# Band attention scores: 128-row products over zero-filled key maps in place of 64-row products

## The reference

```
proj = rmsnorm(h) @ w_in
q (8 heads of 64), k (2 heads of 64), v (2 heads of 64) = the first 768 columns of proj
scores = einsum("bnqkgd,bnskd->bnkgqs", q blocks, k bands) * 64 ** -0.5
scores = scores + bias, masked to |key - query| <= 128
probs  = softmax([scores, sink])[..., :-1]
out    = einsum("bnkgqs,bnskd->bnqkgd", probs, v bands)
```

## Time and profile before

| | |
|---|---|
| median of 3 runs | 2589.55 us (2588.72 to 2590.06) |
| span of the profiled execution | 2587.0 us |
| median less that span (the execution's own time is not printed) | 2.55 us |
| PE busy | 2482.1 us, 96% of the span |
| PE's share of the chain that ended last | 93% |
| share of line L632 (scores) in that chain | 2% |
| the band, 103.8 to 412.9 us | 309.1 us |

### The profile page before, as it was taken

How to read it: one execution, slowest core, us unless ns; L and a number is a source line. 1 busy time by engine, 2 the same in 40 slices (tenths; PEclk the granted TensorE clock), 3 DMA queues, 4 the chain that set the end, 5 groups by cost and what they waited for, 6 DMA issues and landing times.

```text
span 2587.0 us, 33189 instructions
## 1 busy us (share of the span) xinstructions
PE 2482.1 (96%) x13182; PEld 2079.7 (80%) x13182; DVE 991.7 (38%) x1474; ACT 723.0 (28%) x1147; POOL 689.0 (27%) x423
## 2 busy tenths in 40 slices
PE   7999998799989999999999999999999999999997
PEld 5777776699967788888888887888888788887886
DVE  4155633545443421311312235113333353557533
ACT  4134354222321200100101121135444113655022
POOL 2211111343322333433333332311111231111321
PEclk8999998799989999999999998999999999999998
DMA  5211111322331111111111112633441346424422
GB/s 188 96 33 50 33 51 65 74 56 56 119 136 43 34 50 47 49 49 49 49 49 49 49 49 91 219 94 94 115 114 42 133 156 162 116 80 147 146 90 90
DMA packets 247261, 220.54 MB, mean 85 GB/s; under 512 B 42513, under 2 KB 219447, under 8 KB 245608
## 3 DMA queue, kind: packets, MB, share of 16 engines
q1 hardware_dynamic: 225416, 164.36, 22.3%
q10 hardware_dynamic: 21728, 54.57, 5.9%
HBM read 161.12 MB, written 59.87 MB: 85 GB/s over the span
## 4 chain that ended last, share of the span: by engine, by line
PE 93%; DVE 2%; DMA 1%; ACT 1%; POOL 0%; issue 0%; POOLq 0%; ACTq 0%; DVEq 0%; SPq 0%; PEldq 0%; PEld 0%
PE PS L282 40%; PE PS L301 18%; PE PS L1770 4%; PE PS L2420 3%; PE PS L418 3%; PE PS L1725 3%; PE PS L1976 2%; PE PS L632 2%; PE PS L1268 2%; PE PS L1262 2%; PE PS L653 1%; PE PS L1965 1%; PE PS L2259 1%; PE PS L1279 1%; PE PS L641 1%; PE PS L410 1%
## 5 line engine op out<-in xcount | busy, mean ns | idle before, releaser
L253 POOL CAST Wh<-Wraw 128x1024 fp32r<-128x1024 f32 x145 | 151.7, 1046 | 1518.5 <-PE PS L282 643.1
L255 POOL TENSOR_TENSOR Wl<-Wraw,Wh 128x1024 fp32r<-128x1024 f32 x145 | 377.6, 2604 | 20.9
L1644 ACT ACTIVATE rbuf<-PS 128x1024 f32<-128x1024 f32 x32 | 32.9, 1028 | 495.3 <-PE PS L282 484.8
L282 PE MATMUL PS<-Fh,Wh 128*128 128x512 f32 x512 | 157.6, 389 | 0.0
L282 PE MATMUL PS<-Fl,Wh 128*128 128x512 f32 x512 | 157.6, 389 | 0.0
L282 PE MATMUL PS<-Fh,Wl 128*128 128x512 f32 x512 | 157.6, 389 | 0.0
L282 PE MATMUL PS<-XAh,Wh 128*128 128x512 f32 x440 | 140.2, 400 | 8.8 <-POOL Wl L255 6.0
L301 PE MATMUL PS<-XAh,Wh 128*128 128x512 f32 x328 | 136.0, 415 | 2.1 <-POOL Wl L255 2.1
L282 PE MATMUL PS<-XAl,Wh 128*128 128x512 f32 x440 | 136.6, 392 | 0.0
L282 PE MATMUL PS<-XAh,Wl 128*128 128x512 f32 x440 | 136.4, 391 | 0.0
L301 PE MATMUL PS<-XAl,Wh 128*128 128x512 f32 x328 | 135.7, 414 | 0.0
(11 more groups left out here) (429 smaller groups left out, 5419.2 us busy)
## 6 DMA issues: line engine op xcount, KB each, us to landing
Wraw<-in_w_in SPq DMA_DIRECT2D x67, 512.0 KB, 4.1
Wraw<-in_w_ffn_in SPq DMA_DIRECT2D x32, 512.0 KB, 4.0
Wraw<-in_w_ffn_out SPq DMA_DIRECT2D x32, 512.0 KB, 4.0
x_scr<-hT SPq DMA_DIRECT2D x2, 4096.0 KB, 14.2
Wraw<-in_w_out SPq DMA_DIRECT2D x16, 512.0 KB, 4.1
gate_scr<-gbuf ACTq DMA_DIRECT2D x16, 512.0 KB, 2.7
gin<-gate_scr ACTq DMA_DIRECT2D x8, 1024.0 KB, 7.1
xtok<-in_x SPq DMA_DIRECT2D x4, 1024.0 KB, 8.5
```

Source lines behind the costliest of these rows:

```text
L253: pool.tensor_copy(Wh[:, slot], Wraw[:, slot])
L255: pool.tensor_tensor(Wl[:, slot], Wraw[:, slot], Wh[:, slot].bitcast(F32), ALU.subtract).then_inc(w_ready, 1)
L282: mm = pe.matmul(PS[:, 2 * slot + b, :], w[:, slot, k], x[:, b * 512:(b + 1) * 512], start=(c == 0 and m == 0), stop=(c == len(xs) - 1 and ...
```

## The change

The key tile is no longer kept whole. Two maps `kz` of 128 rows are made: map 0 has key head 0 in rows 0 to 63 and zeros in rows 64 to 127, map 1 zeros in rows 0 to 63 and key head 1 in rows 64 to 127. A score product takes the whole query tile (two heads) as stationary operand and the map of its key head as moving operand: the other head meets zeros. The result is the same sum. VectorE writes the zeros, after the split of the activations, and ScalarE waits for them before it copies the keys, now in two instructions of 64 rows. Values move to a tile of their own, `vT`. The semaphore `eps_ok` is renamed `filled` and counts to 3.

```diff
-        attT = sb("attT", [P, 6, S], F32, R + 48)
+        attT = sb("attT", [P, 4, S], F32, R + 48)
+        kz = sb("kz", [P, 2, S], F32, R + 64)
+        vT = sb("vT", [P, S], F32, R + 32)
...
-                    mm = pe.transpose(PS[:, 6 + half, t * P:(t + 1) * P], attT[:, 5, (4 * half + t) * P:(4 * half + t + 1) * P],
+                    mm = pe.transpose(PS[:, 6 + half, t * P:(t + 1) * P], vT[:, (4 * half + t) * P:(4 * half + t + 1) * P],
...
-                rows_ = slice(HD * (h // 4), HD * (h // 4) + HD)
...
-                pe.matmul(PS[:, 2 + u % 2, 0:(hi - lo) * P], attT[rows_, h % 4, n * P:(n + 1) * P],
-                          attT[rows_, 4, lo * P:hi * P], start=True, stop=True).then_inc(w_s, 1)
+                pe.matmul(PS[:, 2 + u % 2, 0:(hi - lo) * P], attT[:, h % 4, n * P:(n + 1) * P],
+                          kz[:, h // 4, lo * P:hi * P], start=True, stop=True).then_inc(w_s, 1)
...
-                act.activation(attT[:, j], pair(j % 2), ACT.Copy, scale=-0.125 if j < 4 else 1.0).then_inc(ps_free, 1)
+                if j < 4:
+                    act.activation(attT[:, j], pair(j % 2), ACT.Copy, scale=-0.125).then_inc(ps_free, 1)
+                elif j == 4:
+                    act.wait_ge(filled, 3)
+                    act.activation(kz[0:HD, 0], pair(0)[0:HD], ACT.Copy)
+                    act.activation(kz[HD:P, 1], pair(0)[HD:P], ACT.Copy).then_inc(ps_free, 1)
+                else:
+                    act.activation(vT[:], pair(1), ACT.Copy).then_inc(ps_free, 1)
...
             split_dve(dve, 0, pv[:, V_MIX:V_MIX + KT], pair(3))
+            dve.drain()
+            dve.memset(kz[HD:P, 0], 0.0).then_inc(filled, 1)
+            dve.memset(kz[0:HD, 1], 0.0).then_inc(filled, 1)
```

More of the change, by code:

```diff
@@ L423, in build @@
         const_in, vec_in, x_in = sem("const_in"), sem("vec_in"), [sem(f"x_in{i}") for i in range(4)]
-        par_in, eps_ok = sem("par_in"), mixer_sem("eps_ok")
+        par_in, filled = sem("par_in"), mixer_sem("filled")
         xT_done, xT_act, xT_dve = sem("xT_done"), sem("xT_act"), sem("xT_dve")
@@ L490, in act_phase0 @@
                 if half:
-                    act.wait_ge(eps_ok, 1)
+                    act.wait_ge(filled, 1)
                     act.activation(ss[:, 0:NT], ss[:, 0:NT], ACT.Sqrt, scale=1.0 / D, bias=eps[:, 0:1]).then_inc(root_done, 1)
@@ L500, in dve_phase0 @@
             dve.memset(eps[:, 0:1], EPS)
-            dve.memset(eps[:, 1:2], SUBLN_EPS).then_inc(eps_ok, 1)
+            dve.memset(eps[:, 1:2], SUBLN_EPS).then_inc(filled, 1)
             for g in BY_DVE:
```

## The result

| | before | changed | |
|---|---|---|---|
| median of the runs | 2589.16 us (4 runs) | 2568.64 us (4 runs, 2566.55 to 2569.56) | ratio 0.9918, 95% interval 0.9904 to 0.9932 |
| span of the profiled execution | 2587.0 us | 2564.8 us | -22.2 us |
| that execution's own time | not printed | 2566.55 us | |

The change is faster by 20.5 us, 0.8%. I had forecast 2565.1 us and a range of 2561 to 2570: the sign, the mechanism and the range held, the size was 24.5 us where 20.5 were found.

What follows compares the result with a forecast made beforehand. PE was taken to bound the kernel, busy throughout stage 1's band (103.8 to 412.9 us). 62 visits to 64-row scores at 0.395 us save 24.5 us, other terms 0: 2589.55 - 24.5 = 2565.1 us, range 2561 to 2570.

Steps and rivals of the forecast that it cites:

- What bounds the kernel: Stage 1's band, 103.8 to 412.9 us: PE busy 309.09 of 309.10 us, so what PE saves there the kernel saves.
- The stop belongs to the row count: At the scores on PE: the loss comes from changing row count, not from plain float32 beside split products; 0.40 us per visit.
- 0.395 us per visit: From the last values instruction through a score to the second filling product: 0.98 us instead of 1.38 without row changes.
- Into a plain float32 product: Step from the last values instruction to the score's first pass with 128 rows on both sides: 0.11 us.
- later stages: End of stage 1 and stages after it move forward as a whole; 2 us allowed both ways.
- rival "half": Only one side of each score is repaired, or the softmax chain limits shorter units: 12 us saved, 2577 us; chance 0.04.
- 62 of 63 visits: Scores in the band: the first visit gives nothing, its transposes wait for the first exponential; 62 visits save 24.5 us.
- Zero fills and key copies at nothing: VectorE memsets and ScalarE's second key copy fall into idle time: cost 0; uncovered, 3 us and 1.03 us.
- Shorter units: The band's 64 units go from 4.83 to 4.45 us; exponentials have 5.0 us of slack, so no engine is late.
- nothing: Stall belongs to plain float32 between split products, or loads cannot run ahead under full-height products: 0 saved, 2589.5 us; chance 0.03.
- slower by the clock: More array rows at work lower the band's granted clock to 1.2 GHz; a quarter there gives 2636 us; chance 0.02.

Runs made afterwards that it cites:

- run 1: The changed kernel with the score matmul alone back on its head's 64 rows; maps, zero fills and two key copies stay: 2588.31 us, ratio 0.9999.
- run 2: The changed kernel with heads 4 to 7 back on 64 rows, heads 0 to 3 kept at 128: 2577.74 us, ratio 0.9957.
- run 5: The kernel before, 64-row scores in pairs of units (0,1), (2,3) and so on, each pair on the same rows: 2578.44 us, ratio 0.996.
- run 6: The kernel before, 64-row scores paired, heads reordered so each pair has one score on rows 0 to 63, one on 64 to 127: 2561.54 us, ratio 0.9893.
- run 4: The changed kernel, 128 rows kept, with the scores of two units side by side at every second unit: 2569.07 us, ratio 0.9919.
- run 7: The changed kernel, 128 rows kept, with scores in pairs and heads in the order 0, 4, 1, 5, 2, 6, 3, 7: 2568.86 us, ratio 0.9918.

## Why the prediction was right, and where it was off

- *What bounds the kernel.* Right: what PE saved in the band went to the end of the kernel, 21.5 us in the band against 20.5 of the medians.
- *The stop belongs to the row count.* Right, argued from the earlier trace rows, and shown by runs 1, 2 and 5. The rule of the Trainium skill that the prediction sets against the rows ("TensorE: Matmul & The Clock Gate", Part 3, "The mechanism": loads overlap running matmuls only across row groups) did not hold here: with 128 rows on both sides the filling's load started with the last score pass, at 163.51 us.
- *0.395 us per visit.* This is the term that was mis-sized. 54 of the visits follow the values, and there the stretch went from 1.38 to 1.04 us with 384 keys and from 1.17 to 0.83 with 256, 0.34 for both. What failed is the step "Into a plain float32 product", 0.11 us, taken from L1233, "which is bound by its load as the values are". The recorded distance did come out at 0.11 (163.02 to 163.13), but the second score pass starts 0.38 us behind the first and not 0.32, so the step is worth 0.17: 1.04 = 0.17 + 0.64 + 0.23.

  The distance of two matmul starts was the wrong measure. The recorded start of a 64-column matmul of the values lies 0.06 us behind the start of its own load (before, the last ones start at 163.93 and 163.87), that of a 128-column one 0.11 (L1245: 447.41 and 447.30), though both sorts come 0.11 us apart. From the last values record to the start of the score's second load, at 163.19, it is 0.17 us, and I take this for the moment at which the first pass has its weights and begins; that reading is argued from the rows and not tested.

  8 visits follow instructions of more columns, 7 the transposes of the output and one a filling product. They gave what I had worked out. One behind the transposes: the score's first pass is at 260.88 and the second filling product at 261.76, 0.88 us, and with the 0.11 from the last transpose before it 0.99. (Start and duration on PE.)

```profile
260.44 0.61 PE L665 MATMUL PS<-ident,wO 128*128 128x128 f32 x4
260.88 0.81 PE L633 MATMUL PS<-kz,attT 128*128 128x384 f32 x2
261.24 0.69 PE L301 MATMUL PS<-XBh,Wl 128*128 128x512 f32 x1
261.76 0.40 PE L301 MATMUL PS<-XBh,Wh 128*128 128x512 f32 x1
```

  With 54 visits at 0.34 and 8 at 0.39 the sum is 21.5 us, the shortening of the band. The median missed the forecast by 3.5 us, and 3.0 of them are this term, for which the range had allowed 1.2; it held because it allowed for the later stages and for rival "half" as well. The profiled span missed by less, 2.3 us, since the 1.4 us of luck ahead of the band hid a part.
- *62 of 63 visits.* Right: the wait of PE's loads at the first transposes grew by 0.4 us, which ate the first visit's gain.
- *Zero fills and key copies at nothing.* Right: two memsets of 0.91 us each stand behind the split, and the two key copies after 9.9 us of idle time. By line, VectorE and ScalarE (busy, mean ns, idle before):

```profile
L778 DVE MEMSET kz<- 64x1024 f32 x1 | 0.9, 912 | 0.3 <-issue 0.3
...
L696 ACT ACTIVATE kz<-PS 64x1024 f32<-64x1024 f32 x1 | 1.0, 1025 | 9.9 <-PE PS L282 9.9
...
L697 ACT ACTIVATE kz<-PS 64x1024 f32<-64x1024 f32 x1 | 1.0, 1021 | 0.0
```

- *Shorter units.* Right: no new wait; VectorE's waits for the scores, 164.0 us less the 56.9 ahead of the band, fell from 107.1 to 92.3 us: slack used up, and enough left.
- *The rivals.* "Half", "nothing" and "slower by the clock" did not come: the clock in the band stayed 1.00. What I had left out is that the 64-row form had a use of its own. Half the array was free beside each score, and no row of the kernel before showed two products at once: the only two scores that stood together, the first two, use the same 64 rows.

What stays open: what PE does in the 0.34 us of a visit. The loads show where they go. From the last values record to the score's second load it is 0.31 us before (163.93 to 164.24) and 0.17 after, so about 0.15 us at the first border; from the second score pass to the filling's second load it is 0.52 us before (164.56 to 165.08) and 0.32 after (163.51 to 163.83), about 0.19 at the second. In the loads' own lines, three before and two after:

```profile
163.87 0.19 PEld L653 LDWEIGHTS PS<-wV,wPT 128*128 128x128 f32 x1
164.24 0.19 PEld L632 LDWEIGHTS PS<-attT 64*128 64x128 f32 x1
165.08 0.19 PEld L301 LDWEIGHTS PS<-XBl,Wh 128*128 128x128 f32 x1
...
163.19 0.19 PEld L633 LDWEIGHTS PS<-kz,attT 128*128 128x128 f32 x1
163.83 0.19 PEld L301 LDWEIGHTS PS<-XAh,Wl 128*128 128x128 f32 x1
```

At both borders the first load starts late, some 0.07 us ahead of the modelled end of the matmul before it. The Trainium skill says in "TensorEngine Tiling (Array Packing)", "Key Properties", that a change of tiling mode drains TensorE. The late loads fit that; as the ends of matmuls are modelled, they don't prove that the array was empty. They fit too with a change of the tile within a mode not draining it, since in run 6 the two halves ran together.

## What to carry to other kernels

A single product of 64 rows between full-height ones paid at both borders, and what it paid didn't depend on its length (0.34 us with 384 keys and with 256): fill the rows with zeros, or gather such products so that they share one visit. If two of them can use different halves of the rows, gather them in such pairs: two then take the time of one, which here beat the zero-filled form by 7 us. The price was measured for 64 rows and plain float32 alone. Where matmuls follow each other at the pace of their weight loads, take distances from the starts of loads: where a matmul's record starts behind its load depended on its columns, 0.06 us with 64 and 0.11 with 128.

## What the runs showed of the hardware that was not expected

- Two float32 products of two passes each, one on rows 0 to 63 and one on rows 64 to 127, run in full overlap: 0.84 us to the next product with 384 keys against 1.48 for a pair on the same rows, and 0.84 for a single one. The Trainium skill, "TensorE: Matmul & The Clock Gate", Part 3, has it that products on different row groups run concurrently; these runs agree, for plain float32 too.
- The kernel's time before the band varies by itself: the first score's load started at 103.8 us before and at 102.3 after, 103.0 in run 1, 103.7 in run 4 and 104.2 in run 7, with the order of work on PE up to there the same. What differs is the granted clock: from 20 to 54 us its mean was 0.80 before and in run 4, 0.85 in run 1 and 0.90 after; run 7 had 0.85 there and 0.96 from 54 to 102 us, where the others had 1.00. Why it was granted so is not shown.
